# First stage of a four-layer kernel: contraction in eight steps of 128 rows instead of four of 256

## The reference

```python
cond = silu(c)                                    # c: (1, 1024)
mod = cond @ ada_w[0] + ada_b[0]                  # ada_w: (2, 1024, 3072)
shift, scale, gate = split(mod, 3)
h = x * (1.0 + scale) + shift                     # x: (512, 1024)
u, v, z_a, x_b, z_b = split(h @ e_w_in, ...)      # e_w_in: (1024, 5120)
b = multiscale_pool(x_b, ...) * silu(z_b)         # and so on
```

## Time and profile before

| | us |
|---|---|
| median of 3 runs | 1877.47 (1877.35 to 1878.3) |
| profiled execution | 1876.41 |
| its span | 1874.3 |
| PE busy | 1807.3 (96%) |
| DVE, ACT, POOL busy | 791.5, 746.1, 788.9 |

### The profile page before, as it was taken

How to read it: one execution, slowest core, us unless ns; L and a number is a source line. 1 busy time by engine, 2 the same in 40 slices (tenths; PEclk the granted TensorE clock), 3 DMA queues, 4 the chain that set the end, 5 groups by cost and what they waited for, 6 DMA issues and landing times.

```text
span 1874.3 us, 24002 instructions
## 1 busy us (share of the span) xinstructions
PE 1807.3 (96%) x8798; PEld 1494.8 (80%) x8798; DVE 791.5 (42%) x1388; ACT 746.1 (40%) x1043; POOL 788.9 (42%) x992
## 2 busy tenths in 40 slices
PE   6999999989999999899999999999997999999998
PEld 6788878878788878788888888888965788888886
DVE  5775775367677632623241111103678341111102
ACT  3423331365656542322253344214456453443212
POOL 0375454354101162355335555443443135555351
PEclk9999999999999999999999999999999999999999
DMA  9543565221212132233233343232311133433321
GB/s 314 172 135 90 151 202 183 93 82 37 73 36 73 45 124 90 68 93 132 90 91 90 93 109 112 102 112 82 114 45 45 46 91 90 109 92 90 120 94 67
DMA packets 209320, 190.94 MB, mean 102 GB/s; under 512 B 10475, under 2 KB 189538, under 8 KB 209250
## 3 DMA queue, kind: packets, MB, share of 16 engines
q1 hardware_dynamic: 208608, 189.69, 32.7%
q10 hardware_dynamic: 642, 0.29, 0.1%
HBM read 187.86 MB, written 2.10 MB: 101 GB/s over the span
## 4 chain that ended last, share of the span: by engine, by line
PE 86%; DVE 5%; ACT 3%; POOL 3%; issue 2%; DMA 0%; SPq 0%; ACTq 0%; POOLq 0%; DVEq 0%
PE PS L1820 27%; PE PS L1822 26%; PE PS L1821 26%; POOL w_low L639 2%; PE PS L2168 1%; ACT w_high L743 1%; PE PS L1949 1%; PE PS L2199 1%; POOL w_low L677 1%; DMA ada_raw<-in_ada_w 0%; DVE soft L1775 0%; DVE probs L1773 0%; PE PS L2359 0%; PE PS L2191 0%; PE PS L2190 0%
## 5 line engine op out<-in xcount | busy, mean ns | idle before, releaser
L639 POOL TENSOR_TENSOR w_low<-w_raw,w_high 128x256 fp32r<-128x256 f32 x905 | 701.6, 811 | 841.2 <-ACT w_high L743 841.2
L1820 PE MATMUL PS<-h_high,w_high 128*128 128x512 f32 (+1 forms) x1488 | 560.7, 377 | 15.4 <-DVE h_low L1453 7.0
L1821 PE MATMUL PS<-h_low,w_high 128*128 128x512 f32 (+1 forms) x1488 | 553.7, 372 | 0.0
L1822 PE MATMUL PS<-h_high,w_low 128*128 128x512 f32 (+1 forms) x1488 | 553.6, 372 | 0.0
L743 ACT ACTIVATE w_high<-w_raw 128x2048 fp32r<-128x2048 f32 (+2 forms) x150 | 280.2, 1868 | 683.8 <-PE PS L1822 669.1
L1820 PEld LDWEIGHTS PS<-h_high,w_high 128*128 128x128 f32 x1488 | 281.6, 189 | 68.6 <-DVE h_low L1453 8.3
L1822 PEld LDWEIGHTS PS<-h_high,w_low 128*128 128x128 f32 x1488 | 281.5, 189 | 48.8
L1821 PEld LDWEIGHTS PS<-h_low,w_high 128*128 128x128 f32 x1488 | 281.8, 189 | 45.7 <-issue 0.7
L1363 DVE TENSOR_TENSOR gate_buf<-gate_buf,PS 128x512 f32<-128x512 f32 x44 | 30.3, 688 | 334.9 <-ACT gate_buf L876 334.3
L1183 DVE TENSOR_TENSOR w_low<-w_raw,w_high 128x2048 fp32r<-128x2048 f32 (+1 forms) x15 | 33.3, 2220 | 325.4 <-ACT w_high L743 325.4
L1820 PE MATMUL PS<-w_high,ff_high 128*128 128x512 f32 x352 | 137.2, 390 | 0.1
(11 more groups left out here) (310 smaller groups left out, 2574.8 us busy)
## 6 DMA issues: line engine op xcount, KB each, us to landing
w_raw<-in_f_gate_up SPq DMA_DIRECT2D x88, 512.0 KB, 4.9
w_raw<-in_f_down SPq DMA_DIRECT2D x40, 512.0 KB, 4.3
w_raw<-in_e_w_in SPq DMA_DIRECT2D x32, 512.0 KB, 5.0
gains<-in_ada_w SPq DMA_DIRECT2D x16, 1024.0 KB, 5.2
w_raw<-in_a_w_in SPq DMA_DIRECT2D x24, 512.0 KB, 4.5
w_raw<-in_o_w_in SPq DMA_DIRECT2D x20, 512.0 KB, 4.3
ada_raw<-in_ada_w SPq DMA_DIRECT2D x8, 1024.0 KB, 13.3
w_raw<-in_e_w_out SPq DMA_DIRECT2D x16, 512.0 KB, 5.6
```

Of the source, the lines that this page charges most:

```text
L639: ins = nc.gpsimd.tensor_tensor(WL[s][:, piece], raw[s][:, piece], WH[s][:, piece].bitcast(F32), ALU.subtract)
L1820: mm(dst, lh, rh, start=first, stop=False, skip_group_check=True)
L1821: mm(dst, lh, rl, start=False, stop=False, skip_group_check=True)
L1822: return mm(dst, ll, rh, start=False, stop=last, skip_group_check=True)
```

## The change

The stage goes over eight chunks of 128 contraction rows (one kt each) and six column tiles (768 columns to split). The tail is chunk 8 and has two tiles (2048 columns to split, 48 matmuls, banks 6 and 7). Step kt needs one load of ada_w, with 128 columns of shift and the 128 of scale that belong to it side by side, in two transfers with runs of 512 bytes; the first is cut in halves of contraction rows. DVE adds the bias for one kt at a time; of the next step's terms the first half stands ahead of the low part of h, the second half behind it. x comes in four column quarters (runs of 1 KB) between the other loads; PE turns it four transposes at a time, always in bank 6, within the step before (after tile 1), and the column stands after tile 2. xT and the ACT copies to it are gone; ACT reads the bank. The load of gmlp_ws (256 KB) moves on ACT's queue from the start to behind the first step. Numbers of the later chunks move by four. All chunks from the tail on are split low by POOL, as before.

```diff
--- before.py
+++ after.py
...
-    ("front", 7, (2, 2)),
+    ("front", 9, (2, 2)),
...
-ADA_FIRST = 2 * K // 2
-ADA_ORDER = (0, 4, 1, 5, 2, 6, 3, 7)
-XB_TILES = 7
+XB_TILES = 6
-FRONT_SIZE = [2 * XB_DEEP] * 4 + [K * P] + [CHUNK] * 9
-ZB_AT, V_AT, POOL_AT = 5, 9, 13
+FRONT_SIZE = [XB_DEEP] * K + [CHUNK] * 10
+ZB_AT, V_AT, POOL_AT = 9, 13, 17
...
-        ada_raw = [dz(f"ada_raw{c}", 2048 * c, [P, CHUNK]) for c in range(ADA_FIRST)]
+        ada_raw = [dz(f"ada_raw{n}", 2048 * n, [P, CHUNK]) for n in range(K)]
-        xT = dz("x_turned", 18432, [P, K, S])
...
-        ada_full = [sem(f"ada_full{c}") for c in range(ADA_FIRST)]
+        ada_full = [sem(f"ada_full{n}") for n in range(K)]
+        ada_half = sem("ada_half")
-        x_in = [sem(f"x_in{t}") for t in range(T)]
+        x_in = [sem(f"x_in{j}") for j in range(K // 2)]
...
             def front(c, pieces):
-            def first_ada(n):
-                c = ADA_ORDER[n]
-                sp.dma_start(ada_raw[c][:, :].rearrange("p (k n) -> p k n", n=256), ada_w[0][:, :, c * 256:(c + 1) * 256]).then_inc(ada_full[c], 16)
-            def load_xb(j):
-                s = j % 2
-                front(j, [(raw[s][:, d * XB_DEEP:(d + 1) * XB_DEEP], w_in["e_w_in"][:, 2 * j + d, 3 * D:3 * D + XB_DEEP]) for d in range(2)])
+            def first_ada(n, ks, done):
+                dst = ada_raw[n][:, :].rearrange("p (k m c) -> p k m c", m=2, c=P)
+                for m in range(2):
+                    sp.dma_start(dst[:, ks, m, :], ada_w[0][:, ks, m * D + n * P:m * D + (n + 1) * P]).then_inc(done, 16)
+            def load_x(j):
+                c = slice(j * 2 * P, (j + 1) * 2 * P)
+                sp.dma_start(x[:, :, c], a["x"].rearrange("(t p) d -> p t d", p=P)[:, :, c]).then_inc(x_in[j], 16)
+            def load_xb(kt):
+                h = XB_DEEP // 2
+                front(kt, [(raw[kt % 2][:, d * h:(d + 1) * h], w_in["e_w_in"][:, kt, 3 * D + d * h:3 * D + (d + 1) * h]) for d in range(2)])
             def load_zb(q):
...
-            first_ada(0)
-            first_ada(1)
+            first_ada(0, slice(0, K // 2), ada_half)
+            first_ada(0, slice(K // 2, K), ada_full[0])
+            load_x(0)
-            for t in range(T):
-                sp.dma_start(x[:, t, :], a["x"][t * P:(t + 1) * P, :]).then_inc(x_in[t], 16)
-            for j in range(1, 4):
-                first_ada(2 * j)
-                first_ada(2 * j + 1)
-                load_xb(j)
-            tail = raw[0][:, 0:K * P].rearrange("p (k c) -> p k c", c=P)
-            front(4, [(tail[:, j:j + K // 2, :], w_in["e_w_in"][:, j:j + K // 2, 3 * D + XB_DEEP:4 * D]) for j in (0, K // 2)])
+            for n in range(1, K):
+                first_ada(n, slice(0, K), ada_full[n])
+                if n % 2 == 0:
+                    load_x(n // 2)
+                load_xb(n)
+            front(K, cols(0, w_in["e_w_in"], 3 * D + XB_DEEP))
...
                 if name == "front":
-                    for c in range(4, 2 * pairs):
+                    for c in range(K, 2 * pairs):
                         if c != ZB_AT:
...
             for n in ("ln_g", "ln_b"):
-            act.dma_start(ws_sb, a["gmlp_ws"].rearrange("h t s -> t h s")).then_inc(rest_in, 16)
...
             def front_high(c):
-            def x_turned(kt):
+            def modulated(kt):
+                act.wait_ge(mod_ready, kt + 1)
-                nact(xT[:, kt, :], PS[:, kt, :], ACT.Copy).then_inc(xt_free, 1)
-            def modulated(kt):
-                act.wait_ge(mod_ready, kt // 2 + 1)
-                scale, bias = mod[:, K + kt:K + kt + 1], mod[:, kt:kt + 1]
-                if kt < 2:
-                    act.wait_ge(xt_tr, kt + 1)
-                    nact(h_tmp[kt % 4], PS[:, kt, :], ACT.Identity, scale=scale, bias=bias).then_inc(xt_free, 1)
-                    act.wait_ge(xt_free, kt + 1)
-                else:
-                    if kt == 2:
-                        act.wait_ge(xt_free, K)
-                    if kt >= 4:
-                        act.wait_ge(hx_low, kt - 3)
-                    steps.link(nact(h_tmp[kt % 4], xT[:, kt, :], ACT.Identity, scale=scale, bias=bias))
+                if kt >= 4:
+                    act.wait_ge(hx_low, kt - 3)
+                nact(h_tmp[kt % 4], PS[:, 6, :], ACT.Identity, scale=mod[:, K + kt:K + kt + 1], bias=mod[:, kt:kt + 1]).then_inc(xt_free, 1)
+                act.wait_ge(xt_free, kt + 1)
-            front_high(0)
-            modulated(0)
-            modulated(1)
-            for kt in range(2, K):
-                x_turned(kt)
-            for j in range(1, 4):
-                front_high(j)
-                modulated(2 * j)
-                modulated(2 * j + 1)
-            front_high(4)
+            for kt in range(K):
+                front_high(kt)
+                modulated(kt)
+                if kt == 0:
+                    act.dma_start(ws_sb, a["gmlp_ws"].rearrange("h t s -> t h s")).then_inc(rest_in, 16)
+            front_high(K)
             def xb_out(f):
                 if f < XB_TILES - 1:
                 elif f == XB_TILES - 1:
-                    act.wait_ge(used[1], BASE["front"].use[1] + 2)
+                    act.wait_ge(used[1], BASE["front"].use[1] + K // 2)
                 else:
-                    act.wait_ge(used[0], BASE["front"].use[0] + 3)
+                    act.wait_ge(used[0], BASE["front"].use[0] + K // 2 + 1)
             def zb_gate(q):
...
-            def first_terms(n):
-                c, part = ADA_ORDER[n], ada_part[n % 4]
-                dve.wait_ge(ada_full[c], 16)
-                if n >= 4:
+            def first_terms(n, ks):
+                part = ada_part[n % 4]
+                if n == 0:
+                    dve.wait_ge(*((ada_half, 32) if ks.start == 0 else (ada_full[0], 32)))
+                elif ks.start == 0:
+                    dve.wait_ge(ada_full[n], 32)
+                if n >= 4 and ks.start == 0:
-                w = ada_raw[c][:, :].rearrange("p (k n) -> p k n", n=256)
-                for k in range(K):
+                w = ada_raw[n][:, :].rearrange("p (k c) -> p k c", c=256)
+                for k in range(ks.start, ks.stop):
                     if k < 2:
...
-            def of_step(ap, j):
-                return ap.rearrange("p (a k) -> p a k", a=2)[:, :, 2 * j:2 * j + 2]
-            for j in range(4):
-                first_terms(2 * j)
-                first_terms(2 * j + 1)
-                split_low("front", j // 2, j % 2, FRONT_SIZE[j])
-                dve.wait_ge(ada_done, 2 * j + 2)
-                v.tensor_tensor(of_step(mod[:, 0:2 * K], j), of_step(PS[:, 7, 256:256 + 2 * K], j), of_step(vec[:, 0:2 * K], j),
-                                ALU.add).then_inc(mod_ready, 1)
-                for kt in (2 * j, 2 * j + 1):
-                    dve.wait_ge(hx_high, kt + 1)
-                    v.tensor_tensor(hL[:, kt, :], h_tmp[kt % 4], hH[:, kt, :].bitcast(F32), ALU.subtract).then_inc(hx_low, 1)
+            def both(ap, kt):
+                return ap.rearrange("p (m k) -> p m k", m=2)[:, :, kt:kt + 1]
+            head, rest_k = slice(0, K // 2), slice(K // 2, K)
+            first_terms(0, head)
+            for kt in range(K):
+                first_terms(kt, rest_k)
+                split_low("front", kt // 2, kt % 2, XB_DEEP)
+                dve.wait_ge(ada_done, kt + 1)
+                v.tensor_tensor(both(mod[:, 0:2 * K], kt), both(PS[:, 7, 256:256 + 2 * K], kt), both(vec[:, 0:2 * K], kt), ALU.add).then_inc(mod_ready, 1)
+                if 0 < kt < K - 1:
+                    first_terms(kt + 1, head)
+                dve.wait_ge(hx_high, kt + 1)
+                v.tensor_tensor(hL[:, kt, :], h_tmp[kt % 4], hH[:, kt, :].bitcast(F32), ALU.subtract).then_inc(hx_low, 1)
+                if kt == 0:
+                    first_terms(1, head)
             def ada_terms(pos):
...
             def first_column(n):
-                c = ADA_ORDER[n]
                 for m in range(2):
                     for j in range(2):
-                        ins = mm(PS[:, 7, 256 + 2 * c + m:257 + 2 * c + m], ada_part[n % 4][:, j, m * P:(m + 1) * P], one_col, start=(j == 0), stop=(j == 1))
+                        c = 256 + K * m + n
+                        ins = mm(PS[:, 7, c:c + 1], ada_part[n % 4][:, j, m * P:(m + 1) * P], one_col, start=(j == 0), stop=(j == 1))
+            def turn_x(kt):
+                if kt % 2 == 0:
+                    pe.wait_ge(x_in[kt // 2], 16)
+                for t in range(T):
+                    ins = tr(PS[:, 6, t * P:(t + 1) * P], x[:, t, kt * P:(kt + 1) * P], ident)
+                ins.then_inc(xt_tr, 1)
+            turn_x(0)
-            first_column(1)
-            for t in range(T):
-                pe.wait_ge(x_in[t], 16)
-                for kt in range(K - 1):
-                    ins = tr(PS[:, kt, t * P:(t + 1) * P], x[:, t, kt * P:(kt + 1) * P], ident)
-                    if t == T - 1:
-                        ins.then_inc(xt_tr, 1)
```

(42 more changed lines are left out.)

## The result

| | us |
|---|---|
| kernel before, median of 11 runs | 1876.66 (1875.12 to 1878.48) |
| changed kernel, median of 11 runs | 1882.20 (1879.54 to 1884.49) |
| ratio | 1.0026, 95% interval 1.0018 to 1.0034 |
| changed kernel, profiled execution and its span | 1882.20, 1880.4 |

Slower by 0.26%, 5.5 us.

The account below looks back on a forecast made before the run. TensorE, busy 96% of the span, bounds the kernel. An 8.1 us earlier start is outweighed by slow clock, turns, waits and clock fall: balance +4.4, by stretch +5.1, on median 1877.47 gives 1882.6 us; range 1876.5 to 1887.5.

Parts of the forecast that it names:

- First matmul: Start of the first stage: its first matmul at 15.9 us instead of 23.95, a head start of 8.1 us.
- Step 0: First of the stage's eight steps: matmuls at the slow clock, 8.6 us (7.6 to 9.3).
- Steps 1 to 6: The six following steps of the stage: a period of 6.15 us each, with a 0.55 us wait, 36.9 in all.
- Step 7: Last step of the stage ahead of the tail: starts at 61.4 us, with 4.2 us of PE work.
- The tail's wait: Ahead of the tail, PE waits for the split of its doubled weights: a new wait of 3.8 us (3 to 6).
- The clock's fall: In the tail, after that pause: eight matmuls of 0.43 us in place of 0.23, costing 1.6 us.
- Zb: Gate chunk behind the tail: its first matmul at 82.0 us against 76.91, +5.1 us.
- Behind zb: Rest of the program after the gate chunk's first matmul: shifts as a whole, second chunk nothing or up to 1 us.
- the first: Rival on the tail's pause: same waits, but the clock holds or the pause is under 3 us; +3.5, 1881.0; chance 0.26.
- bytes: Rival in the stage's steps: slower 512-byte pieces make each step 0.65 us longer, +5 on top, 1887.5; chance 0.10.
- A fall in every step: Rival in the stage's steps: the clock falls at each wait, 1.6 us each, seven cost 11, 1893; chance 0.04.
- The dense stream: Rival over the stage: step waits, tail's wait and clock fall don't arise; -4.2 us, 1873.3; chance 0.07.

Follow-up runs that it names:

- e4: Changed kernel with PE turning the identity 22 times in the idle hole ahead of the tail; 1881.67 us, 1.0021 to the kernel before.
- e6: Changed kernel with the load of gmlp_ws back at the start, as in the kernel before; a single run, first matmul 17.34 us.
- e10: Changed kernel with only the tail mended: split shared by VectorE and GpSimd, PE starting on VectorE's half; 1878.93 us, 1.0003 to the kernel before.
- e3: Changed kernel with the turn of x and the column one tile earlier in each step; 1878.21 us, 1.0005 to the kernel before.
- e2: Changed kernel with PE turning the identity 24 times ahead of x's first turn and 18 behind the first column; 1880.82 us, 1.0018 to the kernel before.
- e9: e8 without its turning of the identity; 1874.85 us, 0.9978 to the kernel before.
- e5: Changed kernel with the first stage's ada_w loaded in 1 KB runs, so shift and scale are wrong columns; 1881.44 us, 1.0025 to the kernel before.
- e8: e7 with PE starting the tail on VectorE's half of the split; 1873.15 us, 0.9976 to the kernel before.
- e11: Kernel before with PE turning the identity 32 times ahead of its first column and 18 behind it; a single run, 1876.37 us.
- e1: Changed kernel with the low split of the tail shared between VectorE and GpSimd; 1879.40 us, 1.0012 to the kernel before.
- e7: Changed kernel with e1, e2 and e3 together, 36 identity turns behind the first column in place of 18; 1878.13 us, 1.0004 to the kernel before.

## Why the prediction was right

Forecast 1882.6, median 1882.20. The forecast put +5.1 us on a median of 1877.47 from three runs; the eleven gave 1876.66, so the difference to compare is 5.5. By its own steps, in the profile:

- **First matmul** 15.9, measured 15.47, with the weights landed at 10.98 (11.4 forecast) and the addition at 12.96 (13.3). The other profiles of kernels with this start have 16 to 17.2: how early the first tiles land varies by over 1.5 us from run to run (x's first turn is at 9.92 here, at 11.60 in e4).
- **Step 0** was the term that was mis-sized. I put the rise of the clock at 3.5 to 6.5 us into the unbroken work (the upper end is from the earlier trace rows; the lower had no row) and 8.6 us for the step. The clock rose 9.3 us after the first matmul and the step took 9.93: the nine matmuls behind the column were slow too, took 3.5 us and outlasted the 2.7 us of chain that the sum had there. In e4, e6 and e10 the step took 7.6 to 8.1. Against 6.08 for a quick step the slow clock cost 1.5 to 3.9 us, where I had 2.4.
- **Steps 1 to 6** 6.15, measured 6.08, with the wait per step as read from the earlier trace rows. There were six such waits, not seven, as slow step 0 hid the first. e3 shows that nine matmuls of cover were the cause: with twelve the holes are gone.
- **Step 7** at 61.4, measured 61.90.
- **The tail's wait** 3.8, measured 3.02 (3.2 by the spacing). The gate terms that I had slowing GpSimd's last three pieces came at 68.30, so at most two pieces met them: 5.64 us for eight.
- **The clock's fall** 1.6, measured 12.59 - 11.01 = 1.58 (changed kernel less e4); e4 shows its cause.
- **Zb** at 82.0, measured 81.88. Step 0's miss (+1.3) and the smaller ones (-0.4, -0.4, -0.6) cancelled. That is luck in the sum, not in the mechanism.
- **Behind zb** I took all to shift as a whole, with up to 1 us at zb's second chunk. That chunk is split in time, but the changed kernel has a hole of 1.40 us ahead of v's first chunk, where the kernel before has none (its matmul there starts at 122.63, 0.23 us behind the one ahead of it). Its timelines of VectorE, ScalarE and PE:

```profile
102.33 0.35 DVE L1206 TENSOR_SCALAR gate_sum<-gains,csil 128x256 f32<-128x256 f32 x1 [7.74 <-DMA gains<-in_ada_w]
...
115.69 1.06 ACT L806 ACTIVATE pool_high<-pooled 128x1024 fp32r<-128x1024 f32 x1 [8.37 <-DVE pooled L1262]
```

```profile
128.47 0.50 PE L1813 MATMUL PS<-w_high,h_high 128*128 128x512 f32 x1 [1.40 <-POOL w_low L641]
```

VectorE waited 7.74 us for a gate block, whose load stands on SP behind a weight chunk that waits for its buffer; its pooled tile came late, ScalarE waited 8.37 us for that with v's split queued behind it. By landmarks of the two traces the changed kernel is later by 4.97 us at zb, 5.84 at v's first chunk (128.47 for 122.63), 6.17 at the matmul that waits 3.74 us for mod (286.01 for 279.84), 6.97 at 381.32 (374.35), and 6.1 at the end. That is read from the trace; no run took it apart. The same hole is in e2, e9, e10 and e3 (1.96, 1.60, 0.94 and 0.70 us), and it isn't in e4, whose zb begins at the same 79.86 as that of e2: how early zb begins doesn't decide it.

Far behind the stage there is a second difference that no edit touches. From a matmul of the attention part (the one that waits 1.11 us for ScalarE's q_raw) to a later one that waits 1.45 us for VectorE's soft, the profiles of before and of the changed kernel take 94.6 and 93.8 us, those of e2, e3, e5, e6, e8 and e11 93.9 to 94.3; e1, e4, e7, e9 and e10 take 96.6 or 96.7. Windows of before and of e10 over this stretch, with a mean granted clock of 0.98 and of 0.95:

```profile
1352.93:1447.50 94.57, 80.92 (x452) 54.45 (x452) 74.57 (x123) 53.48 (x151) 40.71 (x38) 0.98 0.14 50
```

```profile
1354.03:1450.66 96.63, 83.83 (x452) 56.14 (x452) 74.22 (x123) 53.57 (x151) 40.72 (x38) 0.95 0.15 52
```

PE is busy 2.9 us longer with the same 452 instructions. These 2 to 3 us are as large as what most experiments are worth, and the profile of e4 and that of the changed kernel fall on different sides. So a single span doesn't price an edit here; the starts within the stage do, and the medians where their intervals are clear of each other. Whether the edits make the longer stretch more frequent isn't shown.

Of the rivals, the first (the clock holds, or the pause ends under 3 us) stood close: the pause was 3.02 us, and e4 and e1 show the stage with the clock held; bytes decided nothing in the changed kernel (e5) but wait behind it (e8). A fall in every step did not come: steps with 0.36 us holes kept 0.23 us matmuls. The Trainium skill, "TensorE: Matmul & The Clock Gate", on oscillation, tells of a kernel whose clock falls at every contraction tile; no run here shows that. The dense stream, which I gave 0.07 and -4.2 us, is what e8 and e9 built on purpose: 0.9976 and 0.9978.

## What to carry to other kernels

When work is cut finer to start earlier, look at what was paid once per piece and is now paid twice as often, and at the last piece: here the tail doubled and moved into the buffer that comes free last, so a chain of 7.6 us stood over 4.2 us of work. Price a pause twice, as wait and as the slower matmuls behind it. Let the consumer start on the half that is ready, and put the short step that begins a chain as early in the cover as its input allows.

## What the runs showed of the hardware

- The clock's rise moved by 6 us between executions of the same start: 9.3 us after the first matmul in the changed kernel, 3.4 in e4 (starts 0.43 us apart until 19.90, 0.23 to 0.34 from 20.61, first matmul at 17.21).
- A pause of 2.20 us was followed by quick matmuls and a fall 1 us later (e2), one of 1.97 us too (e7), while 1.36 us (e1) was not. In the earlier trace rows 2.37 us was without effect, so the length of the pause alone doesn't decide.
- Turning the identity holds the clock or lets it rise: 18 turns in 2.16 us in e2, no fall behind 22 of them in e4, and in e7 a column at the slow level (1.70 us for its eight instructions, 0.95 when quick), then 36 turns, then matmuls 0.23 us apart.
